# Two weight tiles woven column by column, and weight loads at a step of two words

## The reference

```python
h = rmsnorm(x, norm_mix);  z = h @ w_in             # 2048 x 16464, split among mixers A, B, C and gates
o_a = dsa_attention(...)   # indexer picks keys, softmax over the picked ones
o_b = moba_attention(...)  # block-sparse attention, top 3 past blocks and the own block
o_c = retention(...)       # 8 heads, decays, group norm, swish gate
m = sigmoid(g_a) * (o_a @ w_pa) + sigmoid(g_b) * (o_b @ w_pb) + sigmoid(g_c) * (o_c @ w_pc)
x = x + m @ w_out
h2 = rmsnorm(x, norm_ffn)
x = x + (gelu(causal_dwconv3(h2 @ ffn_up)) * (h2 @ ffn_gate)) @ ffn_down    # d_ff = 5504
y = rmsnorm(x, norm_final)
```

## Time and profile before

| | |
|---|---|
| median of the runs | 2384.52 us |
| span of the profiled execution | 2383.5 us |
| TensorE matmul busy | 2351.6 us (99%), 17202 instructions |
| TensorE weight load busy | 2270.1 us (95%), 17202 |
| VectorE busy | 1410.9 us (59%) |
| ScalarE busy | 919.1 us (39%) |
| GpSimd busy | 314.0 us (13%) |
| DMA | 458.69 MB, mean 192 GB/s |

### The profile page before, as it was taken

How to read it: one execution, slowest core, us unless ns; L and a number is a source line. 1 busy time by engine, 2 the same in 40 slices (tenths; PEclk the granted TensorE clock), 3 DMA queues, 4 the chain that set the end, 5 groups by cost and what they waited for, 6 DMA issues and landing times.

```text
span 2383.5 us, 44504 instructions
## 1 busy us (share of the span) xinstructions
PE 2351.6 (99%) x17202; PEld 2270.1 (95%) x17202; DVE 1410.9 (59%) x2095; ACT 919.1 (39%) x1274; POOL 314.0 (13%) x629
## 2 busy tenths in 40 slices
PE   8999999999999999999999999999999999999997
PEld 8978999999999999998999999999999999999997
DVE  6535568989987545445456645666654356666443
ACT  5334444333333444334333344333333333333332
POOL 1135110000002322333200011000000000000001
PEclk9999999999999999999999999999999999999999
DMA  7448645546557988998776544444445544444553
GB/s 239 143 132 243 178 140 182 180 168 207 204 175 264 307 290 292 302 336 298 245 265 194 183 151 148 153 153 149 152 151 153 150 157 154 148 153 154 149 153 106
DMA packets 174434, 458.69 MB, mean 192 GB/s; under 512 B 25018, under 2 KB 74538, under 8 KB 174096
## 3 DMA queue, kind: packets, MB, share of 16 engines
q1 hardware_dynamic: 141040, 372.31, 47.9%
q0 software_dynamic: 26128, 75.67, 9.7%
q10 hardware_dynamic: 7056, 7.88, 0.9%
HBM read 425.27 MB, written 27.52 MB: 190 GB/s over the span
## 4 chain that ended last, share of the span: by engine, by line
PE 95%; DVE 2%; ACT 1%; issue 1%; DMA 0%; DVEq 0%; SPq 0%; ACTq 0%
PE ps L789 87%; PE ps L1061 1%; PE ps L1014 1%; PE ps L860 1%; PE ps L1044 1%; ACT w_hi L1102 1%; DMA xT<-in_x 0%; PE ps L984 0%; PE ps L976 0%; PE ps L872 0%; PE ps L927 0%; PE ps L963 0%; PE ps L967 0%; PE ps L824 0%; PE ps L902 0%
## 5 line engine op out<-in xcount | busy, mean ns | idle before, releaser
L1353 DVE TENSOR_TENSOR w_lo<-w_raw,w_hi 128x1024 fp32r<-128x1024 f32 (+1 forms) x622 | 749.4, 1207 | 778.3 <-ACT w_hi L1102 775.3
L789 PE MATMUL ps<-h_hi,w_hi 128*128 128x320 f32 x3696 | 1160.6, 314 | 11.7 <-DVE w_lo L1353 9.5
L789 PE MATMUL ps<-h_lo,w_hi 128*128 128x320 f32 x3696 | 1132.3, 306 | 0.0
L789 PE MATMUL ps<-h_hi,w_lo 128*128 128x320 f32 x3696 | 1125.8, 305 | 0.0
L1102 ACT ACTIVATE w_hi<-w_raw 128x1024 fp32r<-128x1024 f32 (+1 forms) x622 | 647.4, 1043 | 802.2 <-PE ps L789 790.5
L789 PEld LDWEIGHTS ps<-h_hi,w_hi 128*128 128x128 f32 x3696 | 694.7, 188 | 41.9 <-issue 38.9
L789 PEld LDWEIGHTS ps<-h_lo,w_hi 128*128 128x128 f32 x3696 | 694.9, 188 | 0.4
L789 PEld LDWEIGHTS ps<-h_hi,w_lo 128*128 128x128 f32 x3696 | 694.5, 188 | 0.0
L789 PE MATMUL ps<-y_hi,w_hi 128*128 128x320 f32 x688 | 213.5, 310 | 1.7 <-DVE yt L1425 1.7
L789 PE MATMUL ps<-y_lo,w_hi 128*128 128x320 f32 x688 | 210.5, 306 | 0.0
L789 PE MATMUL ps<-y_hi,w_lo 128*128 128x320 f32 x688 | 209.2, 304 | 0.0
(11 more groups left out here) (322 smaller groups left out, 2063.4 us busy)
## 6 DMA issues: line engine op xcount, KB each, us to landing
w_raw<-in_w_in SPq DMA_DIRECT2D x258, 512.0 KB, 5.0
w_raw<-in_ffn_up SPq DMA_DIRECT2D x86, 512.0 KB, 3.9
w_raw<-in_ffn_gate SPq DMA_DIRECT2D x86, 512.0 KB, 3.7
w_raw<-in_ffn_down SPq DMA_DIRECT2D x80, 448.0 KB, 3.4
kpg<-in_cache_b_k SPq DMA_DIRECT2D x128, 128.0 KB, 4.5
vpg<-in_cache_b_v POOLq DMA_DIRECT2D x128, 128.0 KB, 5.0
kpg<-in_cache_a_k SPq DMA_DIRECT2D x128, 128.0 KB, 4.8
vpg<-in_cache_a_v POOLq DMA_DIRECT2D x128, 128.0 KB, 4.9
```

Source lines behind the costliest of these rows:

```text
L789: mm = mmul(bank[q][:, 0:T], wp[:, s, cols], xp[:, x.k0 + k, :], start=(x.first and k == 0 and t == 0), stop=(x.last and k == x.nk - 1 and ...
L1353: tt(w_lo[:, s, 0:n], w_raw[:, s, 0:n], w_hi[:, s, 0:n].bitcast(F32), ALU.subtract).then_inc(w_lo_done, 1)
```

## The change

Two neighbouring k tiles of a unit share 256 columns of `w_hi` and `w_lo`: the even tile takes the even columns, the odd tile the odd ones. `w_raw`, filled by DMA, stays in sequence. ScalarE and VectorE therefore read `w_raw` in blocks (pair, tile, column), in the order pair, tile, column, and write `w_hi` and `w_lo` in the same logical order, at a step of two words. The weight load of tile k reads 128 words at a step of two. Units of 7 tiles are rounded up to 8 for the two conversions, and the eighth tile, whatever `w_raw` holds there, is not used.

```diff
+        def paired(x, s, n):
+            return x[:, s, 0:n * P].rearrange("p (a c o) -> p a o c", o=2, c=P)
+        def tile_of(x, s, k):
+            at = k // 2 * 2 * P + k % 2
+            return x[:, s, at:at + 2 * P - 1:2]
+        def in_order(x, s, n):
+            return x[:, s, 0:n * P].rearrange("p (a o c) -> p a o c", o=2, c=P)
+        def even(n):
+            return n + n % 2
...
-                        cols = slice(k * P, (k + 1) * P)
...
-                            mm = mmul(bank[q][:, 0:T], wp[:, s, cols], xp[:, x.k0 + k, :],
+                            mm = mmul(bank[q][:, 0:T], tile_of(wp, s, k), xp[:, x.k0 + k, :],
...
-                n = UNITS[v].nk * P
-                fn(w_hi[:, v % SLOTS, 0:n], w_raw[:, v % SLOTS, 0:n], ACT.Copy).then_inc(w_hi_done, 1)
+                n = even(UNITS[v].nk)
+                fn(paired(w_hi, v % SLOTS, n), in_order(w_raw, v % SLOTS, n), ACT.Copy).then_inc(w_hi_done, 1)
...
-                n, s = UNITS[v].nk * P, v % SLOTS
-                tt(w_lo[:, s, 0:n], w_raw[:, s, 0:n], w_hi[:, s, 0:n].bitcast(F32), ALU.subtract).then_inc(w_lo_done, 1)
+                n, s = even(UNITS[v].nk), v % SLOTS
+                tt(paired(w_lo, s, n), in_order(w_raw, s, n), paired(w_hi, s, n).bitcast(F32), ALU.subtract).then_inc(w_lo_done, 1)
```

## The result

The changed kernel takes 2432.97 us (median of four runs, 2432.46 to 2433.19) against 2384.78 us, a ratio of 1.0200 with an interval of 1.0185 to 1.0214: 48 us slower, where 110 us less were forecast. It lies near the upper end of the range, which went that far only to take in the lower half of rival A. That rival had the right sign, yet its cause is not borne out either, as the experiments show.

The account below looks back on a forecast made before the run. TensorE's 14688 matmul spacings were taken to bound the kernel: 2383.5 - 115 for the loads + 5 for late pages and order effects = 2273.5 us span, put at 2275 us measured, range 2240 to 2440 us.

Parts of the forecast that it names:

- rival A: Weights spread over twice the bytes open more SBUF lines, doubling the stretch: 2504 to 2532 us, less in part; chance 0.19.
- parts (2) and (3): Woven rounding on ScalarE (L1102) and woven subtraction on VectorE (L1353), each put at 0 surcharge.
- I read it as two streams out of SBUF: At L789, moving columns and next weights sometimes want the same place, stretching the spacing 11 ns over the columns' 133.3.
- I take 137 ns: The new spacing from one matmul to the next at L789, near L967's remainder, with 2 ns for first meetings.
- part (1): Weight loads at step 2 (L789): 120 us less over 14688 spacings, 115 us saved after 5 us back.
- The paces: Weights at 8 bytes per 0.81 ns would nearly match the moving tile, so the two streams meet at most at the start.
- the comparison: L967's plain float32 as a case of equal paces: 215 ns each, under 2 ns left over two clocks a column.
- The lower bound of the unknown cost: Lowest new spacing for step-2 loads at L789: 133.3 + 1.7 = 135 ns, the columns and what L967 keeps.
- The 2 ns put down to DMA traffic: Extra sample-stage spacing that comes with heavy DMA traffic and may stay: 2304 x 2.1 = 5 us back.
- B: Rival by the page's rule of independent read ports: no change, 2384 us or a little less; chance 0.09.
- C: Rival of half-rate strided loads: spacing 215 ns or more, some 3410 us; chance 0.05.
- the signs that I had listed for being wrong: Spacing above 150 with loads at 188; loads at 290; w_lo above 2 us with TensorE waiting; or durations as before.

Follow-up runs that it names:

- e11_after_far: Changed kernel with w_hi moved back by 192 bytes and w_lo by 160; 2390.10 us, ratio 1.0014 to 1.0033.
- e9_bench3: Kernel before with 26 groups of 48 equal matmuls behind its last sum, varying moving start, operand and load step; 138.7 ns with one word repeated.
- e3_bench: Kernel before with 44 groups of 48 equal matmuls behind its last sum, varying weight starts, steps and columns; 146.6 ns at nearly every start at step 1.
- e13_map3: Kernel before with 64 groups in the real order behind its last sum, 32 pairs of starts at steps 2 and 1; lowest 144.5 ns, highest 149.0.

## Why the prediction was wrong

**The view of the kernel was right.** TensorE's spacing bounds it, 14688 times, and the loss came as a change of that spacing alone. ScalarE, VectorE and DMA stayed covered, as argued; the 3.5 us of the conversions by themselves are the exception, where parts (2) and (3) had put nothing.

**The step that failed is "I read it as two streams out of SBUF".** From durations that varied between 302 and 314 ns it took the whole 11 ns over the columns' time to be meetings of load and moving operand. The variation was real, and it does hang on places. But it moves the spacing between 144.4 and 151 ns, above a floor that no layout tried here passes: with a quarter of the load it stays at 145.4 ns. The term "I take 137 ns" of part (1), which gave the gain of 120 us, treated that floor as if it could be removed; 147.9 ns was measured, in e11_after_far 144.6 at best. The rows of the kernel before gave no hint of less: its durations went down to 302 ns, but no piece of its chain is below 144.4 ns a matmul.

**The paces were beside the point.** Equal paces gave 147.9 ns, not 137, and no start gave less than 144.4. L967 was misread, too: its four instructions are two matmuls, as each plain float32 matmul leaves two records (48 matmuls left 96 in e9_bench3), so 215 ns is the distance of records. Plain float32 keeps some 3 ns over two clocks a column for a record with loads at a step of 1 and of 2 alike: 48 matmuls of 256 columns took 20.90 and 20.88 us in e3_bench, or 216 ns a record. The bfloat16 group keeps 3 ns at one clock a column, with words of half the bytes. That fits my own reason against the comparison, that L967 asks for half the bytes, but no run tests it by itself.

**The lower bound of the unknown cost was too low, the upper one unused.** 135 ns was a bound of another type of matmul. Measured at a step of 2: 144.5 to 150.5 ns in the groups in the real order, up to 151.0 in a piece of the changed kernel, never near the 215 of half-rate loads. The 2 ns put down to DMA traffic in the sample stage were misread too: groups in silence give the same 146.7, and other pieces of that stage have 13.94 / 96 = 145.2, four of them, one inside the 50 us with the heaviest traffic.

**Parts (2) and (3):** VectorE at 1226 ns was right. ScalarE went from 1057 to 1137 ns, 80 ns more for writing every second word, where L1221 had said none: its runs of 8 words were no stand-in for single words.

**The rivals.** A forecast the sign, and its price was more than twice too high: it doubled a stretch that for the most part does not come from the load's width. Its rule, more openings more meetings, is not borne out either, since at seven of twelve fixed starts a step of 2 added nothing and at (16, 24) the woven kernel equals the old spacing. B, the independent ports of the Trainium skill ("TensorE: Matmul & The Clock Gate", "Step-by-step: what each phase is for"), is closer than I allowed: a quarter of the load gives back only 1 to 5 ns. But it is not exact, as 32 bytes in a buffer's start move the kernel before by 25 us and the step moves it by 48. C's mechanism, a load that bounds the spacing, appears from a step of 3 words on: 174.7 ns at 3, 233 at 4. None of the signs that I had listed for being wrong fits as it stands: A's was a spacing above 150 ns with loads still at 188, and it was 148 to 151 with loads at 195.

**What is shown and what is not.** Shown: the loads make the loss; the spacing depends on step, starts and what went before; the floor is common to both layouts. Not shown: why some starts lead to 144.4 and others to 146.7 or 150 (a phase that each matmul hands to the next would do it, and no run follows one), why a float32r operand whose words differ in place pays 8 ns more than one repeated word, and what the other 5 ns are. A cost of the switch from one load to the next, whatever its width, is not ruled out for them.

## What to carry to other kernels

Before pricing the removal of a stall, find its floor with the suspected cause taken away: 48 equal matmuls behind the last one, with a load of 32 columns beside them, would have shown 145 ns and no gain. A change of stride also changes which addresses meet, so a layout is compared at its own best start (here 256 bytes of starts held a good one for each), and not only at the start where the old layout does well. Two layouts that look 2% apart can both sit on the same floor.

## What the runs showed of the hardware that I had not expected

In no run here did float32r matmuls of 320 columns follow each other in less than 144.4 ns, 11 ns over their columns' time, unless the moving operand repeats one word (138.7); bfloat16 with 256 columns needs 109.4, some 3 ns over. Spacings are not spread evenly: at a step of 1, 19 of the 32 pairs of e13_map3 have 146.6 to 146.8 ns, and four kernels have 146.7 ns in their piece of 2040. A weight load takes 112 ns where it bounds at a step of one word, 118 at two, 173 at three, 233 at four. And 32 bytes in the start of one weight buffer are worth 1% of a kernel that TensorE bounds.
